# Block projections of a hybrid decoder layer as seven products for eight, with the two attentions in alternate halves

## The chip, the cores and the metric

The kernel runs on one core of a Trainium2 chip. The metric is the device time of one launch in microseconds (us), as the median of several runs. TensorE (PE in the profile) does the matrix products, VectorE (DVE), ScalarE (ACT) and GpSimd (POOL) the elementwise work, and SyncE (SP) issues most transfers.

## The reference, cut to what matters

```
h = rmsnorm(x, norm_g)                                  # x: 1024 tokens x 1024
proj = h @ w_in                                         # w_in: 1024 x 10240
sb_q, sb_k, sb_v, sb_z, hg_q, hg_f, hg_i, hg_z, gate_logits = split(proj)   # 8 x 1024, 1 x 2048
# stick-breaking attention, 8 heads of 128:
w[q, k] = sigmoid(z[q, k]) * prod_{k < j < q} sigmoid(-z[q, j]),   z = sb_q sb_k^T / sqrt(128)
u_sb = ((w @ sb_v) * silu(sb_z)) @ w_sb_proj
# HGRN2, 8 heads of 128: forget gates f, keys 1 - f, queries silu(hg_q), values hg_i
S_t = diag(f_t) S_{t-1} + (1 - f_t) hg_i_t^T ;  o_t = S_t^T silu(hg_q_t)
u_hg = (rmsnorm(o, hg_norm_g) * silu(hg_z)) @ w_hg_proj
y = sigmoid(gate_sb) * u_sb + sigmoid(gate_hg) * u_hg
out = rmsnorm(x + y @ w_out, final_norm_g)
```

## The kernel before

Every large product is made of three TensorE products in a rounded fp32 format (fp32r): each operand is split into a high part and the rest, and high x high, high x low and low x high are summed in one PSUM bank. `w_in` comes in panels of 128 columns: `load_panel` brings one (512 KB), ACT copies its high part (`split`, L459), POOL subtracts to get the low part (`w_lo`, L414), and PE multiplies. A panel's product is 1024 tokens x 128 columns over a depth of 1024, which is 8 depth blocks x 2 token halves x 3 = 48 matmuls of 512 columns (`feature_major`, L1063). The two value panels of a head (sb_v, hg_i) are made together with the tokens on the partitions: `token_major` (L1072), 192 matmuls of 256 columns a head.

The work runs in steps, one for each head and two for the gates. Each engine has its own instruction queue, in the order in which the code lists it, and semaphores tie the queues together. A step has 16 slots; in slot `u` PE does one half panel of head `h` (`project`, 24 matmuls of 512 columns or their like), and then pieces of both attentions of head `h-1`, in the slots given by `QK_SLOT`, `TR_SLOT`, `PV_SLOT` and by `attend_hg`: scores of row block `j`, transposes of its weights, weights x values, and the levels of the HGRN2 recursion. Stick-breaking weights are made by two sigmoids on ACT and `weigh` on DVE (two masks, a running product, a multiply). The HGRN2 scores within a chunk of 128 are built by levels: on DVE `prepare_pairs`, `prepare_quads` and `split_product` make the operands that PE sums in `attend_hg` at `u == 0` (L1126, L1127), and then for each level PE multiplies (`L1161`, `L1156`) and DVE scales queries and keys (`grow`: L788, L789) and takes the result. DVE's last work in a step is that preparation; PE wants it after slot 0 of the next step (`pe.wait_ge(sum_step, ...)`).

Per-head buffers are in two sets, so a head's projections are written while the head before is attended. The steps of heads 2 to 7 run in a loop of three rounds of two heads. After the gates, the two branch projections (`branch_panel`) and the output projection (`out_group`) follow, and these the change leaves as they are in their products. The branch inputs and the gates go through HBM (`osb_d`, `ohg_d`, `gate_d`).

Of the kernel before, what the change touches and what calls it, by code (L numbers as in the profile page):

```python
# [12 lines left out]
P = 128  # L33
D = 1024
# [5 lines left out]
SLOTS = 16  # L40
# [4 lines left out]

# [3 lines left out]
CONSTANTS = 9 + 2 * MASKED  # L49
SBUF_BASE = 16512  # L50
# [3 lines left out]
HEAD_PANELS = (SB_Q, SB_K, HG_Q, HG_F, SB_Z, HG_Z, SB_V, HG_I)  # L54
PANEL_SLOT = (0, 1, 0, 1, 0, 1, 2, 3)
GATE_STEP = HEADS
N_GATE_PANELS = 2 * D // P
N_HEAD_PANELS = HEADS * len(HEAD_PANELS)
SB_PANEL0 = N_HEAD_PANELS + N_GATE_PANELS
HG_PANEL0 = SB_PANEL0 + D // P  # L60
OUT_PANEL0 = HG_PANEL0 + D // P
TAIL_SLOT0 = 10 * SLOTS


HEAD_SPLITS = {0: 1, 2: 2, 4: 3, 6: 4, 8: 5, 9: 6, 10: 7, 12: 8}
# [14 lines left out]

NORM_PIECES = [(i, slice(0, D)) for i in range(NT - 1)] + [(NT - 1, slice(0, HALF)), (NT - 1, slice(HALF, D))]


QK_SLOT = {0: 0, 1: 1, 2: 2, 3: 3, 5: 4, 7: 5, 9: 6, 11: 7}
TR_SLOT = {1: 0, 2: 1, 3: 2, 4: 3, 7: 4, 9: 5, 11: 6, 13: 7}
PV_SLOT = {2: 0, 3: 1, 4: 2, 5: 3, 8: 4, 10: 5, 12: 6, 14: 7}


def tr_group(j, part):

    return j if j < 4 else 4 + 2 * (j - 4) + part


def score_banks(j):

    n_banks = 1 if j < 4 else 2
    return n_banks, (j + 1) * P // n_banks
# [8 lines left out]

def build(nc, x, norm_g, w_in, b_gate, lb_logits, hg_norm_g, w_sb, w_hg, w_out, final_g, out):
    ctx = ExitStack()  # L110
    with ctx:
        def sem(name):
            return ctx.enter_context(nc.semaphore(name))

        def place(name, offset, free, dt=F32):
            return nc.alloc_sbuf_tensor_at(name, [P] + list(free), dt, offset=SBUF_BASE + offset)

        KB = 1024

        hT_hi = place("hT_hi", 0, [KT, S], F32R)  # L120
        hT_lo = place("hT_lo", 32 * KB, [KT, S], F32R)
        ohg_hi = place("ohg_hi", 0, [KT, S], F32R)
# [36 lines left out]
        pair_lo = place("pair_lo", at + 8224 + 2048, [HALF], F32R)
        pair_raw = place("pair_raw", at + 8224 + 2048, [HALF])  # L160
        quad_hi = place("quad_hi", at, [S], F32R)
        quad_lo = place("quad_lo", at + 4096, [S], F32R)
        qk_hi = place("qk_hi", at + 8224 + 4096, [S], F32R)
        qk_lo = place("qk_lo", at + 16416, [S], F32R)
        k_lo = [place(f"k_lo{i}", at + 20512 + 4096 * i, [S], F32R) for i in range(2)]
        q_hi = place("q_hi", at + 28704, [P], F32R)
        at += 28704 + 512
# [9 lines left out]
        chunk_total = place("chunk_total", at + 192, [NT])  # L177
        rstd = place("rstd", at + 224, [NT])
        left_ss = place("left_ss", at + 192, [NT])
# [1118 lines left out]
```

## Time and profile before

| | us |
|---|---|
| median of 3 runs (lowest, highest) | 1465.48 (1464.91, 1466.89) |
| span of the profiled execution | 1463.5 |
| PE busy | 1437.1 |
| DVE busy | 788.4 |
| ACT busy | 398.6 |
| POOL busy | 254.6 |

The profile gives the span of the profiled execution from first to last instruction and no other time for it; the median of the runs is 2.0 us above that span. A matmul's "busy" time counts its way through the pipeline, so neighbours overlap: what a matmul costs is the distance between two starts, not its duration. An engine's idle time costs nothing unless PE waits for that engine.

### The profile page before, as it was taken

The page shows a single profiled execution, that of the slowest core. Times are in us where ns is not written, and L with a number is a line of the kernel's source. Part 1 is how long each engine was busy: PE and PEld are TensorE (multiplying, and loading weights), DVE is VectorE, ACT ScalarE, POOL GpSimd, SP SyncE. Part 2 cuts the span into 40 slices and gives each one's busy share as a digit, 9 for nine tenths or more (in the row PEclk, how much of TensorE's full clock was granted, in tenths as well). Part 3 has the DMA queues.
Part 4 walks back from the last instruction along what each step waited for, and adds up shares of the span by engine and source line. Part 5 has one row for each costly group of instructions (what it writes and reads, how often), then busy time and mean ns, then how long its engine had stood idle before and what let it go on. Part 6 is the DMA issues. An engine that isn't in the chain of part 4 may idle for free.

```text
span 1463.5 us, 20990 instructions
## 1 busy us (share of the span) xinstructions
PE 1437.1 (98%) x8312; PEld 1246.5 (85%) x8312; DVE 788.4 (54%) x1157; ACT 398.6 (27%) x637; POOL 254.6 (17%) x126
## 2 busy tenths in 40 slices
PE   7999999999999999999999999999999999999998
PEld 6898898889889788988978988898888888888886
DVE  5145657647656765766666486575450232344413
ACT  7212232232233223223222412332241211001131
POOL 2221210110111111112111201201111222213210
PEclk9999999999999999999999999999999999999999
DMA  6111111120111111111111111202213644433512
GB/s 173 44 58 30 41 53 37 33 62 30 52 37 44 52 37 44 51 30 51 37 45 37 44 51 29 65 30 73 80 65 108 208 124 156 144 94 107 202 44 101
DMA packets 134349, 102.55 MB, mean 70 GB/s; under 512 B 10096, under 2 KB 116592, under 8 KB 134256
## 3 DMA queue, kind: packets, MB, share of 16 engines
q1 hardware_dynamic: 118128, 67.67, 15.5%
q10 hardware_dynamic: 16128, 33.56, 6.5%
q8 instruction: 68, 1.11, 0.3%
q14 instruction: 25, 0.20, 0.0%
HBM read 80.24 MB, written 20.97 MB: 69 GB/s over the span
## 4 chain that ended last, share of the span: by engine, by line
PE 94%; DVE 3%; ACT 2%; issue 1%; POOL 0%; ACTq 0%; DVEq 0%; POOLq 0%
PE banks L1063 56%; PE banks L1072 13%; PE banks L1264 6%; PE banks L1117 4%; PE banks L1097 3%; PE banks L1161 3%; PE banks L1107 2%; DVE q_hi L751 1%; PE banks L1179 1%; PE banks L1156 1%; PE banks L1181 1%; PE banks L1174 1%; PE banks L1127 1%; PE banks L1126 1%; ACT w_hi L459 1%
## 5 line engine op out<-in xcount | busy, mean ns | idle before, releaser
L414 POOL TENSOR_TENSOR w_lo<-w_raw,w_hi 128x1024 fp32r<-128x1024 f32 x95 | 229.3, 2414 | 1108.2 <-ACT w_hi L459 1108.2
L1063 PE MATMUL banks<-hT_hi,w_hi 128*128 128x512 f32 x1024 | 407.5, 398 | 5.9 <-issue 2.9
L1063 PE MATMUL banks<-hT_hi,w_lo 128*128 128x512 f32 x1024 | 399.9, 391 | 0.0
L1063 PE MATMUL banks<-hT_lo,w_hi 128*128 128x512 f32 x1024 | 398.9, 390 | 0.0
L1063 PEld LDWEIGHTS banks<-hT_hi,w_hi 128*128 128x128 f32 x1024 | 192.5, 188 | 45.2 <-issue 4.8
L1063 PEld LDWEIGHTS banks<-hT_hi,w_lo 128*128 128x128 f32 x1024 | 192.2, 188 | 41.4
L1063 PEld LDWEIGHTS banks<-hT_lo,w_hi 128*128 128x128 f32 x1024 | 192.7, 188 | 37.5
L1072 PE MATMUL banks<-w_hi,hT_hi 128*128 128x256 f32 x512 | 147.1, 287 | 0.0
L1072 PE MATMUL banks<-w_lo,hT_hi 128*128 128x256 f32 x512 | 144.8, 283 | 0.0
L1072 PE MATMUL banks<-w_hi,hT_lo 128*128 128x256 f32 x512 | 144.8, 283 | 0.0
L459 ACT ACTIVATE w_hi<-w_raw 128x1024 fp32r<-128x1024 f32 x96 | 101.4, 1056 | 136.1 <-issue 66.3
L1072 PEld LDWEIGHTS banks<-w_hi,hT_lo 128*128 128x128 f32 x512 | 98.2, 192 | 0.0
L1072 PEld LDWEIGHTS banks<-w_hi,hT_hi 128*128 128x128 f32 x512 | 98.2, 192 | 0.0
L1072 PEld LDWEIGHTS banks<-w_lo,hT_hi 128*128 128x128 f32 x512 | 98.1, 192 | 0.0
L768 DVE TENSOR_TENSOR_SCAN kappa<-kappa 128x128 f32<-128x128 f32 (+3 forms) x64 | 86.9, 1358 | 2.2
L751 DVE CAST q_hi<-qT 128x128 fp32r<-128x128 f32 x64 | 31.7, 495 | 88.4 <-ACT kappa L552 84.4
L1117 PE MATMUL banks<-wT,vv 128*128 128x128 f32 x576 | 74.6, 274 | 0.0
L1117 PEld LDWEIGHTS banks<-wT,vv 128*128 128x128 f32 x576 | 72.1, 191 | 2.1
L788 DVE TENSOR_TENSOR hq<-hq,forget 128x512 f32<-128x512 f32 x56 | 62.9, 1124 | 15.9 <-PE banks L1161 14.1
L916 DVE RECIPROCAL scT<-scT 128x1024 f32<-128x1024 f32 x8 | 52.4, 6553 | 29.0 <-ACT scT L567 29.0
L513 ACT ACTIVATE vv<-banks 128x512 f32<-128x512 f32 x32 | 19.1, 597 | 166.5 <-PE banks L1072 166.5
L527 ACT ACTIVATE gate_out<-banks,bg 128x512 f32<-128x512 f32 x32 | 22.1, 689 | 138.7 <-PE banks L1063 138.7
(167 smaller groups left out, 2142.1 us busy)
## 6 DMA issues: line engine op xcount, KB each, us to landing
w_raw<-in_w_in SPq DMA_DIRECT2D x80, 512.0 KB, 3.7
gate_d<-gate_out ACTq DMA_DIRECT2D x32, 256.0 KB, 2.1
gate_in<-gate_d ACTq DMA_DIRECT2D x32, 256.0 KB, 2.7
x_tok<-in_x SPq DMA_DIRECT2D x8, 512.0 KB, 6.0
osb_d<-qT ACTq DMA_DIRECT2D x16, 256.0 KB, 2.0
ohg_d<-hq ACTq DMA_DIRECT2D x16, 256.0 KB, 2.0
osb_raw<-osb_d ACTq DMA_DIRECT2D x8, 512.0 KB, 5.3
w_raw<-in_w_sb_proj SPq DMA_DIRECT2D x8, 512.0 KB, 3.9
```

The costliest lines, as they stand in the source:

```text
L414: nc.gpsimd.tensor_tensor(w_lo[:, slot, :, :], w_raw[:, parity, :, :], w_hi[:, slot, :, :].bitcast(F32), ALU.subtract).then_inc(w_ready, 1)
L459: nc.scalar.activation(w_hi[:, slot, :, :], w_raw[:, parity, :, :], ACT.Copy).then_inc(w_hi_ready, 1)
L751: v.tensor_copy(q_hi[:, :], qT[s][:, tile]).then_inc(q_hi_ready, 1)
L768: v.tensor_tensor_scan(back, back, back, 1.0, ALU.mult, ALU.min).then_inc(scan_done, 1)
L788: v.tensor_tensor(q_odd, q_odd, even.broadcast_to([P, pairs, size]), ALU.mult).then_inc(grown, 1)
L916: v.reciprocal(scT[:, :], scT[:, :]).then_inc(hg_norm, 1)
L1063: last = mm(pj[b], w[:, slot, k, :], halfs(t[:, k, :], b), start=k == 0 and z == 0, stop=k == KT - 1 and z == 2)
L1072: last = mm(dst, hh[:, k, (t + i) * P:(t + i + 1) * P], w[:, 2:4, k, :], start=k == 0 and z == 0, stop=k == KT - 1 and z == 2)
L1097: last = mm(banks[:, 2 + c, 0:m], q, k[s][:, c * m:(c + 1) * m], start=z == 0, stop=z == 2)
L1117: last = mm(attended[:, (j % 4) * P:(j % 4 + 1) * P], vv[s][:, i, 0, :], wT[:, j % 2, i, :], start=i == 0, stop=i == j)
L1161: last = mm(half[0:P - size, n * 64:(n + 1) * 64].rearrange("p (i b) -> p i b", b=size), tile(hk[s], n)[:, 0:P - size], odd, start=True, s ...
L1264: last = mm(dst, y[:, k, i * P:(i + 1) * P], w[:, first:first + n, k, :], start=k == 0 and z == 0, stop=k == KT - 1 and z == 2)
```

## The change

**Seven products for eight.** The transposed, normalized input is held no longer as eight depth tiles of 1024 tokens but as seven combinations of its 2 x 2 blocks (depth halves x token halves), `a_hi[s]` and `a_lo[s]`. Panels are taken in pairs (`HEAD_PAIRS`: q with k, v with z, HGRN2 q with f, i with z; gates two by two, 40 pairs in all). Of a pair, seven combinations `b_hi[s]`, `b_lo[s]` are made from its 2 x 2 blocks (depth halves x panels): POOL forms four sums (`sum_t7`, `sum_t5`, `sum_t6`, `sum_t4`) and seven low parts, ACT seven high parts, all 128 x 512. PE does for each product P1 to P4 12 matmuls of 512 columns (4 depth blocks x 3), in 14 points of 6 matmuls a pair. The results are put together by five DVE additions of a bank to an SBUF tile (`take_u2`, `take_u3`, `take_c22`, `take_c12`, `take_c21`) and two ACT copies. Buffers of the split panel exist once: a part is written anew when the product that read it is done (`freed`).

**Alternate halves.** A head has two half steps of two pairs (28 points). In the first one PE does pieces of HGRN2 of the head before (`HG_AT`), in the second one stick-breaking attention of the same head (`QK_AT`, `TURN_AT`, `PV_AT`). Values now come with the features on the partitions and are transposed (`turn_values`, `turn_inputs`: 16 transposes of 128 x 128 a head). The loop has seven rounds of one head. Queries are split at once instead of by blocks. The gates silu(z) are no longer applied in the heads: z goes to HBM and comes back, and `silu_split` applies it while the gates are projected and after.

```diff
-SLOTS = 16
-HEAD_PANELS = (SB_Q, SB_K, HG_Q, HG_F, SB_Z, HG_Z, SB_V, HG_I)
+P1, P6, P7, P5, P2, P3, P4 = range(7)
+PAIR_BANKS = ((0, 1, 2, 3), (1, 0, 3, 2))
+HEAD_PAIRS = ((SB_Q, SB_K), (SB_V, SB_Z), (HG_Q, HG_F), (HG_I, HG_Z))
+POINTS = 4 * PRODUCTS
+QK_AT = {0: 0, 2: 1, 4: 2, 6: 3, 8: 4, 11: 5, 14: 6, 17: 7}
+TURN_AT = {3: (0, 0), 5: (1, 0), 7: (2, 0), 9: (3, 0), 12: (4, 0), 13: (4, 1), 15: (5, 0), 16: (5, 1),
+           18: (6, 0), 19: (6, 1), 21: (7, 0), 22: (7, 1)}
+PV_AT = {4: 0, 6: 1, 8: 2, 10: 3, 14: 4, 17: 5, 20: 6, 23: 7}
+HG_AT = {0: 0, 2: 1, 5: 3, 8: 4, 10: 5, 13: 6, 15: 7, 18: 8, 20: 9, 22: 11, 25: 12}
...
+            def prepare(n):
+                pool.wait_ge(w_loaded, 32 * n + 32)
+                freed(n, P1)
+                split(n, SPLIT_ORDER, P1, raw_block(0, 0))
+                freed(n, P7)
+                sum_t7(n)
+                split(n, SPLIT_ORDER, P7, part_of(b_sum, P7))
+                freed(n, P5)
+                sum_t5(n)
+                sum_t6(n)
+                freed(n, P6)
+                split(n, SPLIT_ORDER, P6, t2_flat)
+                split(n, SPLIT_ORDER, P5, part_of(b_sum, P5))
+                freed(n, P2)
+                split(n, SPLIT_ORDER, P2, raw_block(1, 0))
+                freed(n, P3)
+                split(n, SPLIT_ORDER, P3, raw_block(1, 1))
+                freed(n, P4)
+                sum_t4(n)
+                split(n, SPLIT_ORDER, P4, part_of(b_sum, P4))
...
+                need(sp, raw_sum, 4 * n)
+                for i in range(2):
+                    sp.dma_start(w_raw[:, i, :, :], by_rows(w_in[0])[:, :, bass.ds(columns[i], P)]).then_inc(w_loaded, 16)
...
+                take_u2(IZ_PAIR, n + 1)
+                weigh(h, 7)
+                take_u3(IZ_PAIR, n + 1)
+                take_c22(IZ_PAIR, n + 1, h)
+                prepare_pairs(h)
+                prepare_quads(h)
+                take_c12(IZ_PAIR, n + 1)
+                split_scores(h)
+                take_c21(IZ_PAIR, n + 1, h)
...
+                for k in ks:
+                    for z, (w, t) in enumerate(((b_hi, a_hi), (b_hi, a_lo), (b_lo, a_hi))):
+                        last = mm(bank, w[:, s, k, :], t[s][:, k, :], start=opens and k == 0 and z == 0,
+                                  stop=k == QUAD - 1 and z == 2, skip_group_check=not opens)
...
+            def first_half(h):
+                for u in range(POINTS):
+                    pair = u // PAIR_POINTS
+                    project(pair, 4 * h + pair, u % PAIR_POINTS)
+                    hg_pieces(h - 1, u)
...
+            with pe.Fori(0, HEADS - 1) as i:
+                first_half(i + 1)
+                second_half(i + 1)
```

At the start the seven combinations of the input are made: DVE has eight operations of 128 x 2048 in a row (four sums, four low parts), ACT four copies of that size, POOL two additions; the first pair's products P5, P7, P6 and P3 wait for them.

SP loads a pair's two panels when POOL has formed the last sum of the pair before (`need(sp, raw_sum, 4 * n)`).

What POOL does for panels, as the kernel's instruction order has it. Before, in a step (an L414 row for each panel, two for a pair):

```order
L414 TENSOR_TENSOR w_lo<-w_raw,w_hi 128x1024
L413 REGISTER_ALU
L414 TENSOR_TENSOR w_lo<-w_raw,w_hi 128x1024
L413 REGISTER_ALU
L414 TENSOR_TENSOR w_lo<-w_raw,w_hi 128x1024
```

Now, for one pair (`t_72` is `t2`):

```order
L561 TENSOR_TENSOR b_lo<-w_raw,b_hi 128x512 x2
L561 TENSOR_TENSOR b_sum<-w_raw 128x512
L561 TENSOR_TENSOR b_lo<-b_sum,b_hi 128x512
L561 TENSOR_TENSOR b_sum<-w_raw 128x512
L561 TENSOR_TENSOR t_72<-w_raw,b_sum 128x512
L561 TENSOR_TENSOR b_lo<-t_72,b_hi 128x512
L561 TENSOR_TENSOR b_lo<-b_sum,b_hi 128x512
L561 TENSOR_TENSOR b_lo<-w_raw,b_hi 128x512 x2
L561 TENSOR_TENSOR b_sum<-w_raw,t_72 128x512
L561 TENSOR_TENSOR b_lo<-b_sum,b_hi 128x512
```

Two operations of 1024 elements a partition become eleven of 512 for each later pair; the `x2` at the head of the piece takes in the last operation of the pair before.

DVE at the end of a step, the preparation of HGRN2 for the first head. Before (`hq_72`, `hk_74`, `forget_76` are the first set of queries, keys and forget gates):

```order
L808 TENSOR_TENSOR scT<-hq_72,hk_74 128x1024
L818 TENSOR_TENSOR hq_72<-hq_72,forget_76 128x1024
L808 TENSOR_TENSOR pair_raw<-hq_72,hk_74 128x512
L803 TENSOR_SCALAR pair_hi<-pair_raw 128x512
L805 SCALAR_TENSOR_TENSOR pair_lo<-pair_raw,pair_hi 128x512
L788 TENSOR_TENSOR hq_72<-hq_72,forget_76 128x512
L789 TENSOR_TENSOR hk_74<-hk_74,forget_76 128x512
L797 TENSOR_TENSOR forget_76<-forget_76 128x512
L808 TENSOR_TENSOR kappa<-hq_72,hk_74 128x512 x2
L803 TENSOR_SCALAR quad_hi<-kappa 128x1024
L805 SCALAR_TENSOR_TENSOR quad_lo<-kappa,quad_hi 128x1024
L803 TENSOR_SCALAR qk_hi<-scT 128x1024
```

Now (`z_out` is written by `take_c22` and, after the piece, by `take_c12`; then come `qk_hi`, `qk_lo` and `turn_in`):

```order
L1001 TENSOR_TENSOR z_out<-banks,u_76 128x512
L1001 TENSOR_TENSOR scT<-hq,hk 128x1024
L1001 TENSOR_TENSOR hq<-hq,forget 128x1024
L1001 TENSOR_TENSOR pair_raw<-hq,hk 128x512
L1131 TENSOR_SCALAR pair_hi<-pair_raw 128x512
L1133 SCALAR_TENSOR_TENSOR pair_lo<-pair_raw,pair_hi 128x512
L1001 TENSOR_TENSOR hq<-hq,forget 128x512
L1001 TENSOR_TENSOR hk<-hk,forget 128x512
L1001 TENSOR_TENSOR forget<-forget 128x512
L1001 TENSOR_TENSOR quad_raw<-hq,hk 128x512 x2
L1131 TENSOR_SCALAR quad_hi<-quad_raw 128x1024
L1133 SCALAR_TENSOR_TENSOR quad_lo<-quad_raw,quad_hi 128x1024
```

The preparation is the same list of operations; what moved is that it now stands behind the addition that takes product P5 of the step's last pair.

PE at the start of a loop round, where it wants that preparation (before: the last matmuls of slot 0; `qk_hi` is what DVE made):

```order
L1063 MATMUL banks<-hT_hi,w_hi 128x512
L1063 MATMUL banks<-hT_lo,w_hi 128x512
L1063 MATMUL banks<-hT_hi,w_lo 128x512
L1126 MATMUL banks<-qk_hi,mean_w 128x512
L1127 MATMUL banks<-qk_lo,mean_w 128x512
```

Now, behind the loop, for the last head (in the loop four register rows stand ahead of the first `mean_w` row):

```order
L1485 MATMUL banks<-a_hi_49,b_hi 128x512
L1485 MATMUL banks<-a_lo_56,b_hi 128x512
L1485 MATMUL banks<-a_hi_49,b_lo 128x512
L1485 MATMUL banks<-a_hi_49,b_hi 128x512
L1485 MATMUL banks<-a_lo_56,b_hi 128x512
L1485 MATMUL banks<-a_hi_49,b_lo 128x512
L1566 MATMUL banks<-qk_hi,mean_w 128x512
L1567 MATMUL banks<-qk_lo,mean_w 128x512
```

In front of the first `mean_w` product there are now six matmuls of the new step where there were 24.

## Rows read from the trace of the kernel before

**Rows 1.** The page: busy us (share of the span) and instructions of each engine.

```profile
PE 1437.1 (98%) x8312; PEld 1246.5 (85%) x8312; DVE 788.4 (54%) x1157; ACT 398.6 (27%) x637; POOL 254.6 (17%) x126
```

**Rows 2.** Groups of PE, one of three alike: busy us, mean ns, idle before.

```profile
L1063 PE MATMUL banks<-hT_hi,w_hi 128*128 128x512 f32 x1024 | 407.5, 398 | 5.9 <-issue 2.9 <-ACT qT L506 2.1 <-DVE hT_lo L723 0.9
```

**Rows 3.** Timeline of PE, 14 matmuls in a row, first and last: start, us.

```profile
1119.68 0.39 PE L1063 MATMUL banks<-hT_hi,w_hi 128*128 128x512 f32 x1
...
1122.63 0.39 PE L1063 MATMUL banks<-hT_lo,w_hi 128*128 128x512 f32 x1
```

**Rows 4.** Timeline of PE, 27 value matmuls in a row, first and last.

```profile
456.24 0.28 PE L1072 MATMUL banks<-w_lo,hT_hi 128*128 128x256 f32 x1
...
459.36 0.28 PE L1072 MATMUL banks<-w_hi,hT_lo 128*128 128x256 f32 x1
```

**Rows 5.** Waits of PE: us in total, times, longest.

```profile
PE banks L1063 <- issue: 2.9, 2, 1.5
```

**Rows 6.** Timeline of PE, the transposes of the input's two halves.

```profile
7.30 6.33 PE L1045 MATMUL banks<-ident,x_tok 128*128 128x128 f32 x32 [7.30 <-POOL level_mask L406]
...
27.25 3.66 PE L1045 MATMUL banks<-ident,x_tok 128*128 128x128 f32 x32
```

**Rows 7.** Groups of POOL: the low parts, and a memset of 128 elements.

```profile
L414 POOL TENSOR_TENSOR w_lo<-w_raw,w_hi 128x1024 fp32r<-128x1024 f32 x95 | 229.3, 2414 | 1108.2 <-ACT w_hi L459 1108.2
L374 POOL MEMSET mean_w<- 128x128 f32 x1 | 0.2, 206 | 0.0
```

**Rows 8.** Timelines of POOL and DVE where they meet, and DVE alone.

```profile
163.97 2.88 POOL L414 TENSOR_TENSOR w_lo<-w_raw,w_hi 128x1024 fp32r<-128x1024 f32 x1 [14.21 <-ACT w_hi L459]
163.90 0.68 DVE L788 TENSOR_TENSOR hq<-hq,forget 128x512 f32<-128x512 f32 x1
396.16 2.39 POOL L414 TENSOR_TENSOR w_lo<-w_raw,w_hi 128x1024 fp32r<-128x1024 f32 x1 [13.58 <-ACT w_hi L459]
396.79 2.31 DVE L788 TENSOR_TENSOR hq<-hq,forget 128x512 f32<-128x512 f32 x1 [1.42 <-PE banks L1161]
407.80 0.68 DVE L788 TENSOR_TENSOR hq<-hq,forget 128x512 f32<-128x512 f32 x1
...
409.61 0.22 DVE L797 TENSOR_TENSOR forget<-forget 128x32 f32<-128x32 f32 x1
```

**Rows 9.** The same two engines; DVE reads a PSUM bank and one SBUF tile.

```profile
365.41 2.40 POOL L414 TENSOR_TENSOR w_lo<-w_raw,w_hi 128x1024 fp32r<-128x1024 f32 x1 [25.60 <-ACT w_hi L459]
365.63 1.23 DVE L858 TENSOR_TENSOR scT<-banks,ident 128x1024 f32<-128x1024 f32 x1 [4.21 <-PE banks L1127]
```

**Rows 10.** Timelines of DVE and PE: a step's preparation, and where PE reads it.

```profile
473.24 1.23 DVE L808 TENSOR_TENSOR scT<-hq,hk 128x1024 f32<-128x1024 f32 x1
...
480.90 0.69 DVE L803 TENSOR_SCALAR quad_hi<-kappa 128x1024 fp32r<-128x1024 f32 x1
...
484.09 1.23 DVE L805 SCALAR_TENSOR_TENSOR qk_lo<-scT,qk_hi 128x1024 fp32r<-128x1024 f32 x1
...
489.57 0.39 PE L1126 MATMUL banks<-qk_hi,mean_w 128*128 128x512 f32 x1
```

**Rows 11.** Groups of DVE: a bank with an SBUF tile; two SBUF tiles.

```profile
L989 DVE TENSOR_TENSOR y_sum<-banks,gate_in 128x512 f32 x16 | 11.0, 688 | 18.5 <-PE banks L1063 18.5
L818 DVE TENSOR_TENSOR hq<-hq,forget 128x1024 f32<-128x1024 f32 x8 | 9.8, 1225 | 0.3
```

**Rows 12.** Group of ACT: the input's high parts out of PSUM.

```profile
L479 ACT ACTIVATE hT_hi<-banks,ng 128x512 fp32r<-128x512 f32 x16 | 9.5, 708 | 0.8 <-PE banks L1045 0.8
```

**Rows 13.** DMA issues: KB each, median us from issue to landing.

```profile
w_raw<-in_w_in SPq DMA_DIRECT2D x80, 512.0 KB, 3.7
```

**Rows 14.** Group of DVE: the reciprocals of HGRN2's norm.

```profile
L916 DVE RECIPROCAL scT<-scT 128x1024 f32<-128x1024 f32 x8 | 52.4, 6553 | 29.0 <-ACT scT L567 29.0
```

**Rows 15.** Timeline of DVE, the output of HGRN2, first and last of six.

```profile
457.03 0.74 DVE L910 TENSOR_SCALAR hq<-banks,hgn 128x512 f32<-128x512 f32 x1
...
459.86 0.69 DVE L913 TENSOR_TENSOR sq_lo<-scT,sq_hi 128x512 fp32r<-128x512 f32 x1
```

More of the change, by code:

```diff
@@ L79, in out_panel, with turn_group @@
     return OUT_PANEL0 + e - (1 if e < 2 else 0)
[L83 to L91, printed above, removed]
+def turn_group(j, part):
     return j if j < 4 else 4 + 2 * (j - 4) + part
+TURNS = 12
 def score_banks(j):
@@ L164, in build @@
[L164 to L167, printed above, removed]
+            return nc.alloc_sbuf_tensor_at(name, [P] + list(free), dt, offset=BASE + offset)
+        OPERAND = 16 * KB
+        a_hi = [place(f"a_hi{s}", s * OPERAND, [QUAD, HALF], F32R) for s in range(PRODUCTS)]
+        a_lo = [place(f"a_lo{s}", s * OPERAND + 8 * KB, [QUAD, HALF], F32R) for s in range(PRODUCTS)]
@@ L772, in finish_sb, with take @@
-            def finish_sb(a, b, s):
-                dve.wait_ge(pv_done, 8 * a + 4 * b + 4)
-                v.tensor_tensor(halfs(qT[s], b), attended, halfs(zT[s], b), ALU.mult).then_inc(sb_taken, 1)
-            def grow(a, m, s):
+            def take(n, taken, products, dst, bank, other):
+                dve.wait_ge(product_done, PRODUCTS * n + products)
+                if taken:
+                    dve.wait_ge(block_taken, 5 * n + taken)
+                tt(dst, bank, other, ALU.add).then_inc(block_taken, 1)
@@ new lines, in _ @@
+            take_level(a, 4)
+            take_level(a, 5)
+            take_c12(GATE_PAIR, n)
+            take_level(a, 6)
+            take_c21(GATE_PAIR, n)
+            take_level(a, 7)
+            n += 1
+            take_u2(n, n)
+            take_u3(n, n)
+            carry_states(a)
+            dve.wait_ge(gate_stored[1], 16)
+            take_c22(GATE_PAIR, n)
+            take_output(a)
+            take_c12(GATE_PAIR, n)
+            for i in range(3):
+                invert(a, i)
@@ new lines, in project, with tile, turn_tokens @@
+            def project(parity, n, p):
+                s = p // 2
+                if p % 2 == 0:
+                    product_waits(n, s)
+                last = multiply(pair_bank(parity, s), s, range(2 * (p % 2), 2 * (p % 2) + 2), s <= P5)
+                if p % 2 == 1:
+                    last.then_inc(product_done, 1)
+            def tile(t, n):
+                return t[:, n * P:(n + 1) * P]
+            def turn_tokens(half, before_it):
+                need(pe, tok_ready, before_it)
+                for i in range(4):
+                    last = nc.tensor.transpose(tile(attended, i), tile(turn_in, 4 * half + i), ident[:, :])
+                last.then_inc(tok_done, 1)
@@ new lines, in _ @@
+            pe.wait_ge(a_ready, QUAD)
+            first_product(P1)
+            first_product(P2)
+            pe.wait_ge(xn_ready, NT)
+            for k in range(KT):
+                need(pe, a_raw_ready, k - 5)
+                for i in range(4, NT):
+                    last = turn_x(i, k)
+                last.then_inc(xT_done, 1)
+            for s in FIRST_ORDER[2:]:
+                first_product(s)
+            pe.wait_ge(const_made, CONSTANTS)
+            pe.wait_ge(first_taken, 1)
@@ L1263, in out_group @@
                     for z, (y, w) in enumerate(((y_hi, hi), (y_lo, hi), (y_hi, lo))):
[L1264 removed]
+                        last = mm(dst, tile(y[k], i), w[:, first:first + n, k, :], start=k == 0 and z == 0, stop=k == KT - 1 and z == 2)
                 return last
```

1597 lines of the change are left out of this document (982 added, 615 removed).

## The prediction

> **What bounds the kernel now.** I read the page's engine totals first: PE is busy 98% of the span, DVE 54%, POOL 17% [rows 1]. A PE total alone proves little, since matmuls overlap, so I went to the timeline: 13 intervals between the rows of the group take 2.95 us, 0.227 us for a matmul of 512 columns, back to back, not the 0.39 printed as its duration [rows 3]; the value matmuls of 256 columns come every 3.12 / 26 = 0.120 us [rows 4]. Then the waits: in the panels PE waited 2.1 and 0.9 us at the start and 2.9 us in two places for "issue", the back edges of the loop, 1.45 us each [rows 2, 5]. So nearly every microsecond is PE work in a row, and what PE no longer does is time gained, as long as the others keep up. Whether they do is the question here, since the change hands them much more.
>
> **The change part by part.** *PE work.* Away: 3 x 1024 matmuls of the panels [rows 2], 3072 x 0.227 = 697.3, and 1536 value matmuls x 0.120 = 184.3. New: 40 pairs x 84 x 0.227 = 762.7, and 128 transposes at 3.66 / 32 = 0.114 [rows 6], 14.6. Net -104.3 us. Six back edges in place of two: +5.8.
>
> *The start.* After the transposes of the second half of x (30.9 us [rows 6]) ACT takes 12 banks at 0.71 = 8.5 us [rows 12], until about 38, since it can begin a little before they end. Then come DVE's eight operations of 128 x 2048. A DVE operation on two SBUF tiles takes 1.23 at 1024 [rows 11] and 0.68 at 512 [rows 8], so 2.3 at 2048: 18.4, until 56.4; then product P3, 12 x 0.227 = 2.7: 59. PE has work only until about 40 of that. +19 (at least 13, if ACT and DVE interleave; at most 25).
>
> *POOL's chain in the gate pairs.* POOL's low part takes 2.39 us at 1024 [rows 8]; at 512 it is at least half, 1.20, and at most 1.20 plus a whole small operation, 0.2 [rows 7]. I take 1.3. The Trainium skill's page "GPSIMD Engine Reference", section 3 (Performance versus the Vector engine), gives 4497 ns for 2048 elements; with 2395 at 1024 that line would give an estimate of 1.34 at 512. From one last sum (`sum_t4`) to the next there are ten POOL operations (13.0), three stops for an ACT copy of 0.75 (2.3), and the load of two panels: one lands after 3.7 [rows 13], two on one queue after about 6. That is 21.3 us, against 84 x 0.227 = 19.1 of PE. With attention in it a pair has 27 to 28 us of PE and hides this; the last six gate pairs don't: 6 x 2.2 = +13 (0 to 30, if gate stores and fetches slow the loads).
>
> *From the gates to the branches.* `silu_split` is three operations at 1.23 and a cast at 0.69 [rows 10, 11], 4.4 us a tile; three tiles are left after the last product, 13.1; PE has 21 matmuls, 4.8 us, that don't need the last tile, so it waits 8.3. The HGRN2 tiles and the first gate are fetched only behind that, and the first panel's gating is late by about 5. +13 (5 to 25).
>
> These give 1463.5 - 104.3 + 5.8 + 19 + 13 + 13 = 1410.0, if each head went at PE's pace.
>
> *POOL in DVE's way.* This is the part that decides. The same DVE operation that takes 0.68 takes 2.31 when POOL's subtraction runs: it ends 2.94 us after POOL began, so it stood until 0.15 before POOL's end; and when DVE had begun first, POOL took 2.88 for 2.39 [rows 8]. An operation with only one input in SBUF, the other in PSUM, keeps its 1.23 under a running POOL [rows 9]. So each operation with two SBUF tiles (and the casts, of which the widest run in the fast form at 0.69 for 1024 elements) can wait up to 1.15 us for each POOL operation of 1.3. The Trainium skill says the same on the page "SBUF — State Buffer", section "Who interferes with whom": DVE and GpSimd share a port pair as an exclusive lock, held for the whole instruction; by that rule, with which the trace agrees, the change's additions of a bank to a tile are free of it and all its weight splitting is not.
>
> POOL goes from 8 x 2.4 = 19 us a head to 44 x 1.3 = 57 us a head, in bursts that follow PE's products. Three places have no room:
> - *The preparation of HGRN2.* Before, it ran from 473.24 to 485.3, 11.5 us without one operation of 0.6 that lies in it, and PE read it at 489.57, 4 us later, with no POOL operation in between [rows 10]. Now it starts when P5 of the last pair is taken. PE still has 6 points of 1.36, transposes 0.4, weights x values 1.8, the back edge 1.45 and one point: 13.2 us. DVE needs 0.6 + 11.5 + 0.6 = 12.7. That fits by 0.5 without POOL. But P5, P2, P3 and P4 free POOL for just eight operations there (t5, t6, four low parts, t4, and P4's), 8 x 1.15 = 9.2. All of DVE's operations there but two have two SBUF tiles or the fast form. PE waits 8.5 behind its first point, and with it the other 27 points. Bounds 0 and 12; I am near the upper, since DVE always has a next operation waiting. 8 heads: +68.
> - *Levels and output.* DVE's part of a level takes 407.80 to 409.83, 2.0 us [rows 8], three of four operations in reach of POOL; between levels 4 and 5, and 6 and 7, PE has two points, 2.7. The output's six operations take 457.03 to 460.55, 3.5 [rows 15], plus ACT's square of 0.6, against three points, 4.1. One block each is past the slack. I take 1 + 1 + 2 us a head (0 to 8): +32.
> - *Value transposes.* PE wants `take_c21` of pair v, z in point 1 of the second half, and it stands behind three reciprocals of 6.55 / 4 = 1.6 [rows 14]. Counted from the norm's sums: 1.2 + 0.7 + 3 x 1.7 + 0.7 = 7.7, against 6.7 for PE. +1.1, 7 times: +8.
>
> `weigh` meets POOL too, but has 2 to 3 us of room in the second half; I take nothing there (up to 2 us a head). The additions of banks, 200 x 0.69 = 138 us [rows 11], lie beside PE.
>
> Sum: 1410.0 + 68 + 32 + 8 = 1518.0 for the profiled span; the runs' median lies 2.0 above it, so **1520 us**, 3.7% slower.
>
> **The rivals.** *It keeps PE's pace, and is faster.* If POOL's operations fall into DVE's pauses or PE's waits push them there, the preparation costs 0 to 2 a head, the levels 0 to 1: 1410 + 8 + 8 x 2 = 1434, and 1455 with 4 or 5. For it: 12.7 against 13.2 is a fit, and POOL's operations wait for DVE's as well as DVE's for them, which can push some of them past the stretch. Against it: those eight POOL operations are released by the very products that PE runs in that stretch. The point of balance is (1463.5 - 1410.0 - 8) / 8 = 5.7 us of waits a head. Chance 0.24.
>
> *POOL itself is the bound in the heads.* If each POOL operation lets one of DVE's (0.9 on the mean) go first, a pair takes 21.3 + 10 x 0.9 = 30 us for 27.8 of PE: 32 pairs x 2.5 = 80 above 1410, so 1490, and with the start of each chain later still about 1510. Then PE would wait for `b_lo`, not for `qk_lo`. Chance 0.12.
>
> *The waits also cool PE.* The first 32 transposes, after an idle PE, took 6.33 us, the second 32 took 3.66 [rows 6]. If every long wait is followed by 2.7 us of that kind, 8 heads and the end add 25: 1545. Chance 0.12.
>
> *The change gains nothing that can be told* (it lands at the balance): 0.04. My forecast: 0.48, with its own range 1490 to 1550.
>
> **How the numbers follow.** No change can be told from noise within 0.2%, 1462.5 to 1468.4. Faster 0.24, same 0.04, slower 0.72. The range leaves out one in ten on each side: from 1428 (the faster rival's better half) to 1572 (blocks at nearly all their bounds, and a cold PE).
>
> **What would show it.** PE's busy share falls from 98% to near 90%; 3360 matmuls at 0.227; the longest wait of PE in total is the one ahead of the `mean_w` products (L1566) for DVE's `qk_lo`, 8 us in each of 8 heads, in a chain of waits that alternates DVE and POOL; DVE's `hq<-hq,forget` has a mean near 1.3 us for 0.68. A period from head to head near 126 us would bear me out; one near 113, with that wait under 2 us, would prove the lock harmless and me wrong. Waits for `b_lo` in the heads would speak for POOL, a granted clock under 0.95 for the cooling.

## The result, and the profile after the change

| | before | after |
|---|---|---|
| median of the runs | 1465.2 us (4 runs) | 1551.16 us (4 runs, 1550.45 to 1552.15) |
| span of the profiled execution | 1463.5 us | 1549.3 us |
| mean granted clock of TensorE | 0.999 | 0.952 |
| sum of PE's waits (all rows of the view) | 19.9 us | 155.5 us |

The changed kernel is slower: ratio 1.0585, 95% interval 1.057 to 1.060. By the prediction's sum PE has 104.3 us less of work, and it still ends 85.8 us later, so by that sum 190 us came back.

The page of the changed kernel, engine totals and PE's granted clock in 40 slices (answers to [rows 1]):

```profile
PE 1386.4 (89%) x7192; PEld 1152.0 (74%) x7192; DVE 1030.7 (67%) x1210; ACT 523.9 (34%) x876; POOL 731.8 (47%) x490
...
PEclk8899899899899989989989998998999989999999
```

POOL went from 17% to 47% of the span, and DVE from 788 to 1031 us with 5% more instructions; in the first experiment, where POOL's instructions are short, the same DVE instructions take 869 us, so 162 us of the 1031 are standing still. The waits of PE: us in total, times, longest (before the change they were 19.9 us in all, 7.3 of it once at the start and no other row over 4.3).

```profile
PE banks L1566 <- DVE qk_lo L1133: 76.4, 8, 9.7
PE banks L1622 <- DVE sq_lo L1001: 20.7, 8, 2.6
PE banks L1485 <- POOL b_lo L561: 12.2, 7, 3.1
PE banks L1485 <- DVE a_lo L1001: 11.0, 2, 8.3
PE banks L1725 <- POOL w_lo L633: 7.4, 1, 7.4
PE banks L1485 <- DVE a_lo L1013: 6.9, 2, 4.4
PE banks L1476 <- POOL level_mask L551: 6.9, 1, 6.9
PE banks L1529 <- ACT v_tok L649: 5.0, 1, 5.0
PE banks L1725 <- DVE y_sum L1001: 3.4, 1, 3.4
PE banks L1529 <- DVE turn_in L1001: 2.6, 6, 0.4
...
PE banks L1725 <- DVE osb_lo L1001: 1.2, 1, 1.2
```

Half of it is one row: the first HGRN2 product of each head waits 9.55 us for the last operation of the preparation. Timelines of DVE, POOL and PE in that stretch of one head (start, us):

```profile
530.10 0.69 DVE L1001 TENSOR_TENSOR z_out<-banks,u 128x512 f32<-128x512 f32 x1 [3.08 <-PE banks L1485]
...
536.62 1.67 DVE L1133 SCALAR_TENSOR_TENSOR pair_lo<-pair_raw,pair_hi 128x512 fp32r<-128x512 f32 x1
538.22 1.78 DVE L1001 TENSOR_TENSOR hq<-hq,forget 128x512 f32<-128x512 f32 x1
...
545.67 1.63 DVE L1131 TENSOR_SCALAR quad_hi<-quad_raw 128x1024 fp32r<-128x1024 f32 x1
...
549.80 1.22 DVE L1133 SCALAR_TENSOR_TENSOR qk_lo<-scT,qk_hi 128x1024 fp32r<-128x1024 f32 x1
...
536.40 1.34 POOL L561 TENSOR_TENSOR b_lo<-t,b_hi 128x512 fp32r<-128x512 f32 x1 [0.82 <-ACT b_hi L649]
537.89 1.55 POOL L561 TENSOR_TENSOR b_lo<-b_sum,b_hi 128x512 fp32r<-128x512 f32 x1
...
545.42 1.33 POOL L561 TENSOR_TENSOR b_lo<-b_sum,b_hi 128x512 fp32r<-128x512 f32 x1 [0.94 <-ACT b_hi L649]
...
551.35 0.79 PE L1566 MATMUL banks<-qk_hi,mean_w 128*128 128x512 f32 x1 [9.56 <-DVE qk_lo L1133]
551.93 0.63 PE L1567 MATMUL banks<-qk_lo,mean_w 128*128 128x512 f32 x1
552.36 0.63 PE L1566 MATMUL banks<-qk_hi,mean_w 128*128 128x512 f32 x1
```

`pair_lo` takes 1.67 for 0.68: POOL's operation ends at 536.40 + 1.34 = 537.74, and 0.68 before DVE's end is 537.61. POOL's next starts at 537.89 and `hq<-hq,forget` behind it takes 1.78; so they alternate. The whole preparation, 11.5 us before the change [rows 10], here takes from 530.71 to 551.02, 20.3 us. `quad_hi`, a cast in the fast form, stood too (1.63 for 0.69). And PE's first products behind the wait come every 0.43 us, not 0.23. Stretches of the same trace: us, busy time (and count) of PE, PEld, DVE, ACT, POOL, then the granted clock, the DMA share and GB/s:

```profile
541.50:551.30 9.80, 0.29 (x2) 0.00 (x0) 9.66 (x10) 0.63 (x1) 4.32 (x3) 0.69 0.13 46
551.30:555.50 4.20, 4.15 (x10) 3.29 (x11) 0.58 (x2) 0.00 (x0) 0.00 (x0) 0.50 0.86 225
555.50:565.00 9.50, 9.50 (x55) 8.08 (x54) 7.94 (x11) 2.31 (x4) 1.55 (x2) 1.00 0.20 73
```

For 4.2 us after ten idle ones PE stands at its lower level (0.50, that is 1.2 of 2.4 GHz). The Trainium skill, page "TensorE: Matmul & The Clock Gate", Part 1, says that matmuls of 512 columns start 426.7 ns apart at the lower level; by that rule, the trace agrees with 0.43.

### The profile page after: what moved, and what is told of

Its sections match the earlier page's. It is cut to its first block, busy times and chain, and to the rows that moved or that the text cites. A ratio compares the mean times of both kernels' runs of the same rounds, so it can differ in the third digit from the quotient of the medians.

```text
span 1549.3 us, 20867 instructions
## 1 busy us (share of the span) xinstructions
PE 1386.4 (89%) x7192; PEld 1152.0 (74%) x7192; DVE 1030.7 (67%) x1210; ACT 523.9 (34%) x876; POOL 731.8 (47%) x490
## 4 chain that ended last, share of the span: by engine, by line
PE 69%; DVE 15%; issue 8%; POOL 3%; DMA 2%; ACT 2%; SPq 0%; DVEq 0%; POOLq 0%; ACTq 0%
PE banks L1485 33%; PE banks L1725 11%; PE banks L1747 6%; PE banks L1561 3%; PE banks L1542 3%; PE banks L1597 3%; DVE hq L1001 2%; DMA w_raw<-in_w_in 2%; PE banks L1551 2%; POOL b_lo L561 2%; POOL b_sum L561 1%; DVE scT L1252 1%; DVE hk L1001 1%; DVE quad_raw L1001 1%; PE banks L1566 1%
## 5 line engine op out<-in xcount | busy, mean ns | idle before, releaser
L1485 PE MATMUL banks<-a_hi,b_hi 128*128 128x512 f32 x1120 | 467.3, 417 | 30.3 <-POOL b_lo L561 12.2
L1485 PE MATMUL banks<-a_hi,b_lo 128*128 128x512 f32 x1120 | 444.8, 397 | 0.0
L1485 PE MATMUL banks<-a_lo,b_hi 128*128 128x512 f32 x1120 | 444.0, 396 | 0.0
L561 POOL TENSOR_TENSOR b_lo<-w_raw,b_hi 128x512 fp32r<-128x512 f32 x120 | 176.9, 1480 | 383.3 <-ACT b_hi L649 383.3
L1485 PEld LDWEIGHTS banks<-a_hi,b_hi 128*128 128x128 f32 x1120 | 216.0, 193 | 74.6 <-issue 17.9
L561 POOL TENSOR_TENSOR b_lo<-b_sum,b_hi 128x512 fp32r<-128x512 f32 x120 | 192.3, 1603 | 127.9 <-ACT b_hi L649 127.2
L1485 PEld LDWEIGHTS banks<-a_hi,b_lo 128*128 128x128 f32 x1120 | 214.2, 191 | 48.4
L1485 PEld LDWEIGHTS banks<-a_lo,b_hi 128*128 128x128 f32 x1120 | 216.0, 193 | 38.0
L633 POOL TENSOR_TENSOR w_lo<-w_raw,w_hi 128x1024 fp32r<-128x1024 f32 x20 | 48.6, 2437 | 158.1 <-ACT w_hi L649 158.1
L561 POOL TENSOR_TENSOR b_sum<-w_raw 128x512 f32<-128x512 f32 x80 | 115.9, 1450 | 1.4 <-PE banks L1485 1.4
L1566 PE MATMUL banks<-qk_hi,mean_w 128*128 128x512 f32 x16 | 11.4, 710 | 76.4 <-DVE qk_lo L1133 76.4
```

The lines of the kernel that those rows point to most:

```text
L561: return nc.gpsimd.tensor_tensor(dst, a, b, op)
L633: nc.gpsimd.tensor_tensor(lo, w_raw[:, t % 2, :, :], hi.bitcast(F32), ALU.subtract).then_inc(panel_ready, 1)
L1485: last = mm(bank, w[:, s, k, :], t[s][:, k, :], start=opens and k == 0 and z == 0, stop=k == QUAD - 1 and z == 2, skip_group_check=not opens)
```

## The experiments

Theory T: DVE and POOL don't run side by side where both have their operands in SBUF, POOL's new work lies in the stretch that PE waits for, and each wait also costs PE its clock. All ratios are to the kernel before (1465.4 to 1466.4 in these comparisons); "the changed kernel" has 1551.2.

### POOL's operations made short

```diff
+                if few:
+                    dst, a, b = dst[:, 0:32], a[:, 0:32], b[:, 0:32]
                 return nc.gpsimd.tensor_tensor(dst, a, b, op)
...
```

> From the second pair on, each of POOL's eleven operations of a pair covers 32 of its 512 columns, and the block products P4, P5 and P7 get a standing tile for their weights instead of the sums (so the sums and most of the low parts are left out); the order, the semaphores and the work of ACT, DVE and PE are as in the changed kernel. Theory (DVE waits for POOL's instructions): the wait of PE for qk_lo falls from 9.55 us a head to 1.5 or less, the one for sq_lo from 2.6 to under 0.5, DVE's hq<-hq,forget goes from 1.19 us on the mean to about 0.7, the period of a head from 129.5 to 113 to 115, and the waits for b_lo of the gate pairs vanish (12 us): 1551 - 8 x 15.5 - 12 = about 1415, between 1405 and 1430. Rival (the stretch is too long and starts too late on DVE whatever POOL does): the wait for qk_lo stays over 5 us a head, and the time over 1480.

1420.5 us, ratio 0.969 (0.968 to 0.971). The period of a head is 116.65 for 129.6. PE's waits, and the group of DVE of the expectation (busy us, mean ns | idle before):

```profile
PE banks L1574 <- DVE qk_lo L1141: 10.4, 8, 1.3
...
PE banks L1630 <- DVE sq_lo L1009: 1.9, 8, 0.3
```

```profile
L1009 DVE TENSOR_TENSOR hq<-hq,forget 128x512 f32<-128x512 f32 x56 | 38.9, 695 | 62.6 <-PE banks L1605 44.3 <-PE banks L1601 18.3
```

In the changed kernel that group has 1043 ns. But it had no free 0.68 before the change either:

```profile
L788 DVE TENSOR_TENSOR hq<-hq,forget 128x512 f32<-128x512 f32 x56 | 62.9, 1124 | 15.9 <-PE banks L1161 14.1
```

There its median is 686 ns and its longest 2887: POOL met the levels then too, and PE hardly waited for it. So this mean alone is no measure of the harm; what counts is which operation meets POOL, and here it is the preparation.

Order, semaphores and DVE's work are as they were, so the rival (length and late start) is worth 1.3 us a head of the wait for `qk_lo`. POOL's instructions are worth 131 us in all, and not all of that is DVE standing: 66.0 are the wait for `qk_lo` and 18.8 the one for `sq_lo`, 12.2 are PE's own wait for POOL's `b_lo` in the gate pairs, and 110 intervals at the lower clock fewer make 22 more. The run is also about what the seven products would be worth if weights cost POOL next to nothing: 3.1% faster than before.

### POOL's work raised

```diff
...
+                for i in range(2):
+                    need(pool, again, 2 * (n - 1) + i)
+                    tt(part_of(b_lo, P2), raw_block(1, 0), part_of(b_hi, P2).bitcast(F32), ALU.subtract).then_inc(again, 1)
+                pool.wait_ge(again, 2 * n)
                 split(n, SPLIT_ORDER, P2, raw_block(1, 0))
```

> POOL makes the low part of P2 three times in each pair (two operations of 128 x 512 more, 1.3 us each, released in the stretch in which DVE prepares HGRN2); nothing else is changed. Theory (DVE waits for POOL's instructions): the wait for qk_lo grows by 2 x 1.15 = 2.3 us a head, 18 in all, and POOL's chain in the six last gate pairs by 6 x 2.6 = 16: 1551 + 34 = 1585, between 1573 and 1600. Rival (POOL and DVE only share time while both happen to be busy, and POOL has the room): the wait for qk_lo grows by under 0.5 us a head, only the gate pairs pay: about 1567.

1591.1, ratio 1.086 (1.084 to 1.088): 40 us for 34.

```profile
PE banks L1572 <- DVE qk_lo L1139: 88.8, 8, 11.1
PE banks L1491 <- POOL b_lo L562: 22.0, 8, 3.8
...
PE banks L1557 <- DVE beta L1007: 7.4, 8, 0.9
...
PE banks L1599 <- DVE forget L1007: 6.1, 9, 0.7
```

`qk_lo` grew by 12.4 and `b_lo` by 9.8, and 13.5 came in two places that had had no wait (weights x values, `beta`; levels, `forget`). The direction holds; the two operations cost 1.55 us a head there, not 2.3, and the rest lies where the slack had just been enough.

### DVE's first two operations earlier

```diff
                 take_u3(IZ_PAIR, n + 1)
+                prepare_scores(h)
                 take_c22(IZ_PAIR, n + 1, h)
```

> DVE's first two operations of the preparation (scT<-hq,hk and hq<-hq,forget) move ahead of take_c22 of pair i, z, into the 3.08 us in which DVE waits for product P5. Theory (PE waits for DVE's total of work and of lock in this stretch, so any idle time of DVE that is used counts in full): the wait for qk_lo falls from 9.55 to about 6.6, eight heads give 24 us: 1527, between 1523 and 1537. Rival (POOL's operations are pushed along and come back on DVE's later ones, so the stretch is as long as POOL's work makes it): the wait falls by under 1 us a head, and the time stays over 1543.

1536.5, ratio 1.049 (1.047 to 1.050). The wait for `qk_lo` is 59.9 us in total, 7.5 a head: 2.1 gained for 3.08 of idle time used. Between the two: DVE's idle time was real, but a third of it was lost again to POOL (the two `quad_raw` of a head now take 1.77 each for 1.21, and `scT<-hq,hk` 1.76 for 1.50; `pair_raw` takes 1.17 for 1.65).

### PE kept at work in the wait

```diff
                 if u == 0:
+                    pe.wait_ge(sb_taken, 2 * a + 2)
+                    for i in range(40):
+                        mm(attended, mean_w[:, :], a_hi[P1][:, i % QUAD, :], start=True, stop=True)
                     pe.wait_ge(sum_step, SUM_STEPS * a + SUM_STEPS)
...
-                    pe.wait_ge(sb_taken, 2 * a + 2)
```

> PE runs 40 matmuls of 512 columns (40 x 0.227 = 9.1 us) into an unread bank inside the wait for qk_lo of each head; the rest is as in the changed kernel. Theory (an idle stretch costs PE its clock, and the slow clock behind it lies on the path that sets the end): the first products behind the wait come every 0.23 us instead of 0.43, the granted clock stays over 0.9 there, and each head gives 2.0 us: 1551 - 16 = 1535, between 1532 and 1540. Rival (DVE's levels bound that stretch anyway, so PE's clock costs nothing): the matmuls are quick but the waits behind grow, and the time stays within 1548 to 1553.

1535.1, ratio 1.047 (1.045 to 1.049): 16.1 us for the 16 expected. The same two stretches:

```profile
537.50:547.00 9.50, 9.26 (x41) 7.15 (x39) 9.40 (x9) 0.64 (x1) 4.04 (x3) 1.00 0.13 47
547.00:551.00 4.00, 4.00 (x18) 3.31 (x19) 2.04 (x3) 0.43 (x1) 0.00 (x0) 1.00 1.01 261
```

The clock stays at 1.00, and 18 instructions of PE run in 4.0 us for 10 in 4.2. From the first `mean_w` product of a head to its output wait PE takes 54.0 us for 55.8. So the slow clock is a cost of its own, 1.8 us a head, on the path that sets the end. That the total is no more than 16.1 has a second cause: behind the output wait of 2.6 us the clock now fell in four of the seven heads between 200 and 1000 us, where it had fallen in one, and each such head is 0.7 us longer there.

### HGRN2's pieces later on PE

```diff
-HG_AT = {0: 0, 2: 1, 5: 3, 8: 4, 10: 5, 13: 6, 15: 7, 18: 8, 20: 9, 22: 11, 25: 12}
-I_AT = {3: 0, 4: 1}
+HG_AT = {2: 0, 4: 1, 7: 3, 10: 4, 12: 5, 15: 6, 17: 7, 20: 8, 22: 9, 24: 11, 27: 12}
+I_AT = {5: 0, 6: 1}
```

> All of PE's and ACT's HGRN2 pieces stand two points (2.7 us of PE work) later in the table; DVE's order is unchanged. Theory (the wait for qk_lo is a plain shortfall of cover): it falls from 9.55 to about 6.85 us a head, and nothing behind it comes too late: 1551 - 22 = 1529. Rival (the chain behind it is as tight, so that the delay comes out at the other end): the last piece now stands at point 27, its roots, reciprocals and the value transposes of the second half are 2.7 us late, PE waits for them by 2 to 3 us a head, and the time stays within 1543 to 1555.

1608.1, ratio 1.097 (1.095 to 1.099), 57 us worse than the changed kernel: neither case, and the rival's direction.

```profile
PE banks L1566 <- DVE qk_lo L1133: 55.0, 8, 7.0
...
PE banks L1485 <- DVE k_raw L1001: 18.6, 7, 2.9
...
PE banks L1529 <- DVE turn_in L1001: 15.5, 7, 3.0
PE banks L1485 <- DVE z_out L1001: 14.0, 7, 2.0
```

The aimed wait fell by 2.7 a head, as two points should give. But DVE's queue has the additions of the banks behind the levels, so a later level on PE makes PE wait for its own bank. (All waits together rose by 31.2 of the 57 us; the new ones, of 2 to 3 us, also brought some 80 more intervals at the lower clock, 16 us.) I took the order of DVE's queue for the cause and changed DVE's order to fit (from the fourth level on the pieces were one point late only):

```diff
+                take_c22(pairs[0], n, h)
                 if attend:
                     take_level(a, 3)
-                take_c22(pairs[0], n, h)
...
-                if attend:
-                    take_output(a)
                 take_c12(pairs[1], n + 1)
+                if attend:
+                    take_output(a)
+                    invert(a, 0)
```

> HGRN2 pieces two points later again (from the fourth level on by one), but DVE's order follows: take_c22 stands ahead of level 3, take_c12 ahead of level 5, take_c22 of v, z ahead of carry_states, take_c12 ahead of take_output, take_c21 ahead of three of the four reciprocals. Theory (the loss of 57 us of the run with the shift alone came from banks that stood behind a later HGRN2 piece in DVE's queue): the waits for k_raw, z_out and turn_in (48 us there) vanish, the wait for qk_lo stays near 7: 1551 - 22 = 1529, between 1520 and 1540. Rival (DVE's own chain is as tight as PE's there, and a later first piece makes all behind it late): over 1555.

1605.6, ratio 1.096 (1.094 to 1.098). My reading fell: the three waits went, and others of the same size came.

```profile
PE banks L1565 <- DVE qk_lo L1133: 55.0, 8, 7.0
PE banks L1621 <- DVE sq_lo L1001: 31.7, 8, 4.4
PE banks L1596 <- DVE forget L1001: 28.1, 13, 2.3
```

In both runs a later start moved the wait along the chain of levels, banks and output, all of which pass through DVE, and did not remove it. The last piece alone, one point later (`25: 12` to `26: 12`, and `take_c21` behind two reciprocals for three):

> The last HGRN2 piece (PE's sums over the squares, which wait 2.6 us a head for sq_lo) stands one point (1.36 us of PE work) later, and DVE takes c21 of v, z behind two reciprocals instead of three. Theory (the wait at the output is a shortfall of cover, and behind it there is room): it falls to 1.2 us, eight heads give 11: 1540, between 1537 and 1545. Rival (as in the two runs with later pieces, the reply of DVE behind it then comes late by as much): the time stays within 1548 to 1556, with new waits for turn_in or beta.

1551.2, ratio 1.059 (1.057 to 1.060), no change: `sq_lo` fell from 20.7 to 10.1 us, and `beta`, which had no row, has 10.9. The rival was right here too.

### High parts on ACT

```diff
+                nc.scalar.activation(hi[:, :], raw[:, :], ACT.Copy, scale=float(P)).then_inc(high_made, 1)
...
-                v.tensor_scalar(hi, raw, float(P), None, ALU.mult).then_inc(sum_step, 1)
```

> ACT makes pair_hi, quad_hi and qk_hi (scaled copies) instead of DVE; DVE keeps the low parts, pair_lo behind grow(1), qk_lo ahead of quad_lo. DVE's stretch loses 0.43 + 1.63 + 0.69 = 2.75 us as it stands in the changed kernel's trace. Theory (PE waits for DVE's work and its waits for POOL, in one queue without slack): the wait for qk_lo falls by 2.5 to 3 us a head: 1551 - 22 = 1529, between 1525 and 1535. Rival (the operations taken away were partly time in which POOL held the way, and POOL's instructions then meet DVE's other operations, or ACT comes late with a high part): under 1 us a head, over 1543.

1526.1, ratio 1.041 (1.039 to 1.043): 25 us for 22; the wait, now for `quad_lo`, DVE's last operation there, is 53.8 us in total, 2.8 less a head for 2.75 taken away. DVE's work in the stretch counts in full, with the time that it stands.

### Combinations

> The earlier scores (which alone gave 14.7 us), the shift by two points with DVE's order adapted, and 20 matmuls (4.5 us) in the wait that is left, together. Theory (the three are independent: 14.7 from idle time of DVE used, 22 from cover, 16 from the clock): 1551 - 53 = 1498, between 1490 and 1512. Rival (later pieces leave DVE's queue too full behind them, and what the stretch gains is lost at the output and at the value transposes): over 1520.

1569.2, ratio 1.071 (1.069 to 1.073). It holds the shift, so it inherits its chain (`sq_lo` 31.7, `forget` 20.9); the rival's case.

> The earlier scores (14.7 us alone), the high parts on ACT, the output one point later, and 14 matmuls (3.2 us) in the wait that is left. By the theory 1551 - 15 - 22 - 11 - 14 = 1489, between 1478 and 1503. Rival (the edits share the same slack, POOL's bursts above all, so that they don't add up): over 1510.

1518.3, ratio 1.035 (1.034 to 1.037), 29 above the sum of the parts. Of these, 11 had been put down for the later output, which alone gave nothing. Another cause is in DVE's timeline: with its operations earlier, it waited for a high part that stood in ACT's queue behind the weights' copies.

```profile
529.07 0.69 DVE L1142 SCALAR_TENSOR_TENSOR pair_lo<-pair_raw,pair_hi 128x512 fp32r<-128x512 f32 x1 [4.22 <-ACT pair_hi L815]
```

> Against the changed kernel: the earlier scores; qk_hi and quad_hi on ACT, but pair_hi on DVE again (with all three on ACT, DVE stood 4.22 us a head for pair_hi, behind the weight copies in ACT's queue); 8 matmuls (1.8 us) in the wait that is left; at the output ACT multiplies by the gain (hq<-banks,hgn), so that DVE has 0.75 + 0.74 us less there; at the start 42 matmuls in PE's two longest waits; behind the gates the first panel's high part ahead of the last two sigmoids on ACT, and the tiles of osb one step earlier on DVE. By the theory (every microsecond taken from DVE's queue in a stretch that PE waits for counts in full): 1518 for the run with all highs on ACT, less 8 x 3.8 for its PE stretch (6.4 us of dummies and wait down to 2.6), less 8 x 1.5 at the output, 3.6 at the start and 5 behind the gates: 1518 - 30 - 12 - 4 - 5 = 1467, between 1458 and 1485. Rival (POOL's instructions find DVE's other operations in the stretch, so that the edits only add up by half): over 1490.

1502.0, ratio 1.023 (1.022 to 1.025), 35 above. The 4.22 us of idle time were gone, yet dummies and wait went from 6.1 us a head (14 x 0.23 + 23.5 / 8) only to 5.9 (8 x 0.23 + 32.3 / 8). With DVE packed tighter POOL's burst met other operations (the two `quad_raw` took 3.48 for 2.35): that was the rival. The edit behind the gates cost 5 us (the stretch of the next expectation); PE's waits for `b_lo` rose there to 21.8 us in total, which I put down to `silu_split` meeting POOL in the gate pairs, without a run of its own. DVE has no pause in its stretch any more, and it is as long as DVE's work and its standing for POOL together; the next run takes POOL out of it:

```diff
+                if held:
+                    pool.wait_ge(sum_step, 2 * n)
                 freed(n, P5)
                 sum_t5(n)
...
+                for s in (P6, P5, P2, P3):
+                    split(4 * h + 4, s)
```

> Nothing of the computation is left out. As the combined version, but without the dummy matmuls of the heads and without its reordering behind the gates (which there took 150.0 us from the output wait to the third branch panel, for 145.0 in the changed kernel), and with POOL held back: in the pair q, k of the next head its nine operations from t5 on (and the four copies of ACT that go with them) wait until DVE has made the last low part of the preparation. Theory (a time at which DVE and POOL both want to work costs PE time only in this stretch): DVE's stretch runs in its free durations, the 6.0 us of dummies and wait a head fall to 0.5, PE waits 1.5 for the low part of P6 instead: 1502 - 5 - 8 x 4 = 1465, between 1450 and 1482, the same as before the change. Rival (nine operations of POOL can't be late without being late throughout: their burst meets DVE's levels, and the next pair's loads start late): waits for b_lo over 3 us a head and new waits at the levels, 1495 or more.

1488.5, ratio 1.016 (1.014 to 1.017); the range had said 1450 to 1482. The period of a head is about 122. DVE, POOL and the waits of PE:

```profile
512.24 0.69 DVE L1154 SCALAR_TENSOR_TENSOR pair_lo<-pair_raw,pair_hi 128x512 fp32r<-128x512 f32 x1
512.85 0.69 DVE L1022 TENSOR_TENSOR hq<-hq,forget 128x512 f32<-128x512 f32 x1
...
520.08 1.29 POOL L563 TENSOR_TENSOR b_sum<-w_raw 128x512 f32<-128x512 f32 x1 [8.88 <-DVE quad_lo L1158]
```

```profile
PE banks L1511 <- POOL b_lo L563: 21.0, 16, 3.2
PE banks L1555 <- ACT i_tok L658: 18.3, 8, 2.3
PE banks L1623 <- DVE forget L1022: 8.1, 8, 1.5
```

`pair_lo` and `hq<-hq,forget` run in their free 0.69, and the wait for the preparation has no row any more. But of the 13.5 us against the combined version about 5 come from the reordering behind the gates that was taken back, and the dummies of the heads went too; so holding POOL back gave some 9 us where 32 had been expected. A smaller bill came for the late burst: `b_lo` of P6 (1.15), the token copy on ACT, now behind four weight copies (2.3), and a level. Of the 86 us that the change cost, edits around it that leave the computation whole give back 63; the best of them is still 1.6% slower than the kernel before.

## Why the prediction came out as it did

The forecast of 1520 (3.7% slower) had the right sign, mechanism and place; the 31 us between it and 1551 (1 us outside the forecast's own range of 1490 to 1550) are sizes, and one rival that came true beside it. The sizes were off in both directions and in part cancelled: that the sum came as near as it did is in part luck.

- **PE's work**, -104.3: too large. Inside a row of products 0.227 us holds, but the first interval behind each return from attention's small matmuls is longer, 0.31 on the mean (below), and the changed kernel has 266 such returns for 102. In PE's timelines, without waits and without the lower clock's share, the 3360 products take 804 us (799 in the run with short POOL operations) for the 763 of the sum, and the 3072 before took 712 for 697. With the value matmuls (187 before) and the transposes (12 now), PE's work fell by 82 to 88 us. That run shows it too: 1463.5 - 104.3 with its own waits (56.0 - 19.9) and 51 intervals at the lower clock (10) gives 1405, and its span is 1418.9.
- **Back edges**, +5.8: measured 0. Around the head's seam (540.04 and 540.27 are two of its products) no interval exceeds the usual one. In the traces the loop's branch on PE's queue takes 3.36 and 3.38 us at the two back edges before the change, and 0.21 to 0.24 now; why it is so much shorter is open.
- **The start**, +19: waits for `a_lo` 11.0 + 6.9, less the 3.0 of before, 15; and 33 matmuls at 0.43 us, 7 more: 22. The first head's 5.0 for `v_tok` I had not seen.
- **POOL's chain in the gate pairs**, +13: 12.2. **From the gates to the branches**, +13: 7.4 + 3.4 + 1.2 = 12.0.
- **The preparation**, +68 (8.5 a head): 76.4 (9.55). The 13.2 us that PE was to have for cover were 11.7 (530.10 to 541.79), since 1.45 of them was a back edge that now cost nothing; DVE stood 8.2 us for the 9.2 forecast (20.3 - 11.5 - 0.6). The mechanism and its place are shown by taking POOL's work away, raising it, and moving it in time.
- **Levels and output**, +32 (1 + 1 + 2 a head): levels 0, output 20.7 (2.6). DVE stood idle 0.8 to 2.1 us ahead of the levels in the head read, so it had room to stand; in the run with two more operations 6.1 us of waits for `forget` came up there, so this slack was nearly used up.
- **Value transposes**, +8: 2.6. PE's wait at the output just ahead gives DVE time to catch up, but no run tests that this is why.
- **The waits cool PE**, a rival with 0.12, +25: this step failed, as I had set it beside the forecast, not into it. Of all intervals between matmuls 161 are 0.43 us, with 0.23 they would be 32 us shorter; the run with dummies, in which such stretches vanished in one place and grew in another, gave back 16.1 net. A wait of near 10 us was itself my forecast, so its cold clock belonged to the sum.
- **Balance**: the waits rose by 155.5 - 19.9 = 135.6 and the clock cost 32, of the 190; the 22 us left are PE's work, which fell by 82 and not by 104.

Of the signs named ahead, PE's share (89%), the wait's place and length, and its alternation with POOL came; the head's period was 129.6 for 126; `hq<-hq,forget` has 1043 ns at 512 columns, not near 1300, and its 1124 before the change shows that the sign was badly chosen.

The longer interval behind a return to the products, here in the run with POOL held back (541.89 to 542.21, where the next is 0.23):

```profile
540.29 1.79 PE L1623 MATMUL banks<-hq,hk 128*120 128x64 f32 x16
541.89 0.48 PE L1511 MATMUL banks<-a_hi,b_hi 128*128 128x512 f32 x1
542.21 0.40 PE L1511 MATMUL banks<-a_lo,b_hi 128*128 128x512 f32 x1
542.44 0.39 PE L1511 MATMUL banks<-a_hi,b_lo 128*128 128x512 f32 x1
```

## What to carry to other kernels

A change that takes work from the bounding engine and gives some to a helper must be costed by who the helper meets: here the 82 to 88 us that PE's work fell by were paid back by the 131 us that POOL's new work cost, most of it by meeting DVE (with the cold clock that followed). Look for the one stretch where both queues are released by the same products, and ask whether the helper's burst can be held until the critical queue is through it. Packing the critical queue tighter gained here too, but the edits together gained less than their sum, as the helper's burst then met other operations. To start a tight chain later moved the wait to its next link. And cutting the saved work into smaller pieces costs something by itself: here about 0.09 us at each of some 160 more returns to the products.

## What was not expected of the hardware

- A loop's seam on PE cost 1.45 us in the kernel before and nothing that shows in this one (its branch takes 3.36 to 3.38 us there, 0.21 to 0.24 here).
- ACT was not slowed by either: its copies of 128x512 from SBUF have a mean of 628 to 632 ns in the changed kernel and 628 to 630 ns with POOL's operations short. That fits with high parts moved there paying in full.
- The lower clock behind an idle time of 2.6 us (the output wait) came once in the seven heads between 200 and 1000 us. The same two products and their successors, in two heads of the changed kernel (columns as in the stretches above):

```profile
477.70:481.00 3.30, 3.30 (x15) 2.71 (x16) 1.98 (x2) 2.13 (x4) 0.46 (x1) 1.00 0.39 159
607.30:610.00 2.70, 2.70 (x7) 2.15 (x8) 0.50 (x2) 0.65 (x2) 0.00 (x0) 0.50 0.44 182
```

So the loss behind a short wait can be read from a trace, but it doesn't follow from the wait's length (in the run with dummies it came in four of these seven heads, with the same waits of 2.6 us); behind each wait near 10 us it came every time.
